# Which blocks of a later group have their sums placed on chip: second, fourth, sixth and eighth instead of first, third, sixth and eighth

## The chip, the cores and the metric

One Trainium2 chip, one of its cores. The metric is the device time of one execution in microseconds (us). TensorE is called PE (its weight loads PEld), VectorE DVE, ScalarE ACT, GpSimd POOL and SyncE SP.

## The reference, cut to what matters

One layer of a hybrid diffusion backbone for 384 tokens (128 of context, 256 latent) of width 1024: adaLN, a mixer of two branches, and a mixture of 64 SwiGLU experts (inner width 256, 8 chosen per token) with a shared expert. The change is in the experts:

```
act    = silu(einsum('nd,edf->nef', t, w_gate_e)) * einsum('nd,edf->nef', t, w_up_e) * gates[:, :, None]
routed = einsum('nef,efd->nd', act, w_down_e)
shared = (silu(t @ w_gate_s) * (t @ w_up_s)) @ w_down_s
return (routed + shared).reshape(B, T, D)
```

An expert's gate, up and down weights are 1 MB each in f32; all of them, 192 MB, are read from HBM.

## The kernel before

**Blocks and turns.** The experts are sorted by load and worked in 4 groups (NGRP) of 16 experts, each in 10 blocks (BPG, UN): a heavy block (H) has one expert with up to 128 slots, a light block (L) two experts with 64 slots each. Group 0 runs in the order HHHHLLLLLL (ORDER0), groups 1 to 3, the later ones, in HLLHLHLLHL (ORDER). One pass of one block on all engines is a turn. In turn u PE does (`block_turn`, L1519): gate and up of block u (`gate_up`, L1457), transposes of the next block's tokens (L1454), the down product of block u-1 (`down`, L1471), transposes of the activation (L1541), the slot numbers of block u+3 (L1445) and, if block u-1 is placed, its set of placing products (`place`, L1491). So block v's products stand in turn v+1.

**Two ways out of a block.** The result of a block is one row per slot; rows must be added up per token. A scattered block writes its rows with an indirect accumulating DMA from POOL (L748) into y_dram. A placed block (in later groups alone, `is_placed`, L411, by the tuple PLACED, L45) stays on chip: ACT writes the high part of its rows into y_r (`rows_out`, L1035), DVE makes a 0/1 matrix from the slots' tokens (L2007) and the low part of the rows (`place_low`, L2010), PE multiplies matrix and rows in 12 products (L1503), and DVE adds the 6 results to ffn_acc (`place_sums`, L2021). PE's next gate/up waits until the first of these is out, its next transposes until all are (L1526, L1529). `place_low` of block v waits for the scatter of block v-1, since the two use each other's buffer (L2016); `scatters_ahead` and `places_ahead` (L414, L419) count scatters and sets from PLACED, and `SCATTERED` (L46) follows from it.

**The weights.** SP issues all loads in one order (L549 to L559): in turn u gate and up of block u's experts (`load_gu`, two DMAs of 1 MB each), then down of block u-1 (`load_dn`, one). There are five buffers (RING): the heavy blocks use slot 3 alone, the light experts slots 1, 2, 4 and 0 in turn, so that two light blocks are held. A load waits on SP until the products that read the slot's former weights are done.

**After the last turn** the accumulated rows of y_dram, of the last block and of ffn_acc are added (L1566 to L1574, L2036 to L2059), and the final norm is taken.

Of the kernel before, what the change touches and what calls it, by code (L numbers as in the profile page):

```python
# [41 lines left out]
NBLK = NPASS_BLK * MAXPASS  # L42
NSIDE = 2 * NPASS_BLK
FIXED = 4
PLACED = (0, 2, 5, 7)  # L45
SCATTERED = BPG - len(PLACED)  # L46
HEAVY = 16
EMPTY = 1024
# [16 lines left out]
def hybrid_step(nc, x_prompt, x_sample, cache_k, cache_v, state_f, state_b, c, c_ctx,  # L65
# [5 lines left out]
    with ctx:  # L71
# [336 lines left out]

        assert max(PLACED) < UN - 2 and all(v + 1 not in PLACED for v in PLACED)

        def is_placed(u, first):  # L411
            return not first and u % UN in PLACED

        def scatters_ahead(b, u):  # L414

            back = 1 if u < 0 else 0
            return b * (16 * SCATTERED) + 16 * (len(PLACED) - SCATTERED * back + sum(v not in PLACED for v in range(u % UN)))

        def places_ahead(b, v, each):  # L419

            return b * (each * len(PLACED)) + each * (PLACED.index(v) - len(PLACED))

# [41 lines left out]
        def _(sp):  # L464
# [95 lines left out]

            sp.wait_ge(S["added"], passes * (NGRP * SCATTERED * 16) + 16 * (len(PLACED) - 1))
            sp.sem_inc(S["sp_turn"], 1)
# [1527 lines left out]
```

## Time and profile before

| | |
|---|---|
| three timed runs | 967.43, 969.09, 971.62 us (median 969.09) |
| the profiled execution | 965.96 us, its span 963.7 us |
| PE busy | 883.8 us, 92% |
| DVE, ACT, POOL busy | 413.2, 253.4, 144.0 us |
| SP's DMA queue (q1) | 263.21 MB, 68.7% of the span on 16 DMA engines |
| POOL's DMA queue (q0) | 27.37 MB, 10.0% |
| granted clock of PE, mean | 0.977 |

The experts run from 378 to 928 us of the span, the later groups from 508 us. In the rows, times are microseconds from the span's start. A row of the order of time gives start, duration, engine, line, operation, output and inputs, the count of instructions merged, and in brackets the idle time of the engine before it and what ended it.

### The profile page before, as it was taken

The page shows a single profiled execution, that of the slowest core. Times are in us where ns is not written, and L with a number is a line of the kernel's source. Part 1 is how long each engine was busy: PE and PEld are TensorE (multiplying, and loading weights), DVE is VectorE, ACT ScalarE, POOL GpSimd, SP SyncE. Part 2 cuts the span into 40 slices and gives each one's busy share as a digit, 9 for nine tenths or more (in the row PEclk, how much of TensorE's full clock was granted, in tenths as well). Part 3 has the DMA queues.
Part 4 walks back from the last instruction along what each step waited for, and adds up shares of the span by engine and source line. Part 5 has one row for each costly group of instructions (what it writes and reads, how often), then busy time and mean ns, then how long its engine had stood idle before and what let it go on. Part 6 is the DMA issues. An engine that isn't in the chain of part 4 may idle for free.

```text
span 963.7 us, 12124 instructions
## 1 busy us (share of the span) xinstructions
PE 883.8 (92%) x4170; PEld 514.4 (53%) x4170; DVE 413.2 (43%) x947; ACT 253.4 (26%) x415; POOL 144.0 (15%) x213
## 2 busy tenths in 40 slices
PE   4799998999999999999997999999999999999973
PEld 2387875899897764543333444444443444444431
DVE  1562483577665554233331332432342334233445
ACT  2537623344423240221211111111111111111111
POOL 7300000000001041122132012012102111111112
PEclk9799999999999999999998999999999999999987
DMA  9974778422227197799999999999999999999832
GB/s 341 343 252 182 293 262 239 109 89 79 98 89 297 64 415 316 243 340 390 404 388 386 421 403 400 410 403 394 423 404 398 404 420 401 402 406 414 340 107 101
DMA packets 85320, 295.65 MB, mean 307 GB/s; under 512 B 17370, under 2 KB 33814, under 8 KB 60320
## 3 DMA queue, kind: packets, MB, share of 16 engines
q1 hardware_dynamic: 64400, 263.21, 68.7%
q0 software_dynamic: 12176, 27.37, 10.0%
q10 hardware_dynamic: 8704, 4.54, 2.1%
q8 instruction: 25, 0.41, 0.2%
q14 instruction: 15, 0.12, 0.0%
HBM read 287.16 MB, written 22.81 MB: 322 GB/s over the span
## 4 chain that ended last, share of the span: by engine, by line
PE 67%; DMA 19%; DVE 5%; issue 3%; ACT 2%; SPq 2%; POOL 1%; ACTq 1%; POOLq 0%; DVEq 0%
PE bank L1466 21%; DMA gu<-in_w_up_e_dram 12%; PE bank L1485 10%; PE bank L1090 7%; PE bank L1092 6%; PE bank L1091 6%; DMA y_dram<-y_sb,slot_row 4%; DMA chunk_raw<-in_w_ada_dram 3%; PE bank L1503 3%; PE bank L1454 3%; PE bank L1118 2%; PE bank L1359 2%; PE bank L1159 1%; PE bank L1192 1%; PE bank L1541 1%
## 5 line engine op out<-in xcount | busy, mean ns | idle before, releaser
L1466 PE MATMUL bank<-gu,x_t 128*64 128x512 f32 (+1 forms) x1024 | 286.4, 601 | 12.8 <-DMA gu<-in_w_up_e_dram 11.0
L1466 PEld LDWEIGHTS bank<-gu,x_t 128*64 128x64 f32 (+1 forms) x1024 | 102.6, 151 | 167.7 <-issue 162.2
L1485 PE MATMUL bank<-dn,a_t 128*64 128x512 f32 (+1 forms) x512 | 145.3, 597 | 4.1 <-ACT shared_sb L1016 3.5
L1985 DVE TENSOR_TENSOR act_sb<-silu_sb,bank 128x256 f32<-128x256 f32 x40 | 16.9, 422 | 229.4 <-ACT silu_sb L1059 229.4
L1059 ACT ACTIVATE silu_sb<-bank 128x256 f32<-128x256 f32 x40 | 15.4, 385 | 330.0 <-PE bank L1466 330.0
L748 POOL DMA_INDIRECT y_dram<-y_sb,slot_row x27 | 45.9, 1701 | 306.5 <-DVE slot_row L1875 260.6
L1485 PEld LDWEIGHTS bank<-dn,a_t 128*64 128x64 f32 (+1 forms) x512 | 48.5, 150 | 74.0 <-issue 67.4
L1090 PE MATMUL bank<-h_hi,chunk_lo 128*128 128x384 f32 x240 | 84.6, 353 | 0.0
L1092 PE MATMUL bank<-h_hi,chunk_hi 128*128 128x384 f32 x240 | 81.1, 338 | 0.0
L1091 PE MATMUL bank<-h_lo,chunk_hi 128*128 128x384 f32 x240 | 81.0, 337 | 0.0
L736 POOL DMA_INDIRECT xg<-h_dram,slot_tok x42 | 44.0, 1047 | 179.8 <-DVE slot_row L1875 155.5
L443 DVE TENSOR_TENSOR chunk_lo<-chunk_raw,chunk_hi 128x2048 fp32r<-128x2048 f32 x25 | 57.1, 2287 | 19.4 <-ACT chunk_hi L437 19.3
L1993 DVE COPY a_t<-bank 128x256 f32<-128x256 f32 x40 | 17.0, 424 | 103.9 <-PE bank L1541 103.7
L437 ACT ACTIVATE chunk_hi<-chunk_raw 128x2048 fp32r<-128x2048 f32 x25 | 47.7, 1914 | 49.6 <-PE bank L1092 49.4
L1044 ACT ACTIVATE y_sb<-bank,slot_gate 128x512 f32<-128x512 f32 x56 | 38.5, 687 | 66.6 <-PE bank L1485 63.8
L1454 PEld LDWEIGHTS bank<-ident,xg 128*128 128x128 f32 x328 | 36.4, 141 | 27.9 <-issue 27.9
L1090 PEld LDWEIGHTS bank<-h_hi,chunk_lo 128*128 128x128 f32 x240 | 45.4, 189 | 7.0 <-issue 5.3
L1091 PEld LDWEIGHTS bank<-h_lo,chunk_hi 128*128 128x128 f32 x240 | 45.5, 190 | 0.3
L1092 PEld LDWEIGHTS bank<-h_hi,chunk_hi 128*128 128x128 f32 x240 | 45.5, 189 | 0.0
L2026 DVE TENSOR_TENSOR ffn_acc<-ffn_acc,bank 128x512 f32<-128x512 f32 x72 | 44.1, 682 | 0.4
L1503 PE MATMUL bank<-y_r,place_r 128*128 128x512 f32 x144 | 35.9, 398 | 8.8 <-DVE a_t L1993 6.9
L1454 PE MATMUL bank<-ident,xg 128*128 128x128 f32 x328 | 43.9, 277 | 0.0
(345 smaller groups left out, 1072.7 us busy)
## 6 DMA issues: line engine op xcount, KB each, us to landing
gu<-in_w_gate_e_dram SPq DMA_DIRECT2D x64, 1024.0 KB, 15.7
gu<-in_w_up_e_dram SPq DMA_DIRECT2D x64, 1024.0 KB, 20.8
dn<-in_w_down_e_dram SPq DMA_DIRECT2D x64, 1024.0 KB, 26.0
chunk_raw<-in_w_ada_dram SPq DMA_DIRECT2D x24, 1024.0 KB, 8.9
chunk_raw<-in_w_in_dram SPq DMA_DIRECT2D x18, 1024.0 KB, 5.4
chunk_raw<-in_w_out_dram SPq DMA_DIRECT2D x4, 1024.0 KB, 5.0
y_dram<-zeros POOLq DMA_DIRECT2D x1, 3072.0 KB, 17.6
chunk_raw<-in_w_pa_dram SPq DMA_DIRECT2D x2, 1024.0 KB, 5.0
```

Source lines behind the costliest of these rows:

```text
L437: act.activation(chunk_hi[j % HIGHS][:, :], chunk_raw[slot[n]][:, :], ACT.Copy).then_inc(S["chunk_high"], 1)
L443: dve.tensor_tensor(chunk_lo[slot[n]][:, :], chunk_raw[slot[n]][:, :], chunk_hi[j % HIGHS][:, :].bitcast(F32), ALU.subtract).then_inc(S["c ...
L736: pool.indirect_dma_start(xg[u % 2][:, :], None, h2_dram[:, :], bass.IndirectOffsetOnAxis(ap=slot_tok[:, u % UN:u % UN + 1], axis=0), boun ...
L748: pool.indirect_dma_start(y_dram[:, :], bass.IndirectOffsetOnAxis(ap=slot_row[:, u % UN:u % UN + 1], axis=0), y_sb[u % 2][:, :], None, bou ...
L1090: pe.matmul(out, left[1], right[0], start=start, stop=False)
L1091: pe.matmul(out, left[0], right[1], start=False, stop=False)
L1092: return pe.matmul(out, left[0], right[0], start=False, stop=stop)
L1454: mm = pe.transpose(bank[k // 4][:, (k % 4) * P:(k % 4 + 1) * P], xg[u % 2][:, k * P:(k + 1) * P], ident[:, :])
L1466: mm = pe.matmul(bank[2 + u % 2][at_x, :].rearrange("p (g n) -> p g n", g=2), x_t[:, cols], wide[:, :, k, :], start=(k == 0), stop=(k == K ...
L1485: mm = pe.matmul(bank[5 + half][at_x, :], a_t[:, cols], dn[slot_of(x, first)][:, wc], start=(k == 0), stop=(k == 1))
L1503: return pe.matmul(out[:, :], place_r[:, t * P:(t + 1) * P], y[:, halves[half]], start=start, stop=not start)
L2026: dve.tensor_tensor(ffn_acc[t][:, cols], ffn_acc[t][:, cols], out[:, :], ALU.add).then_inc(S["place_out"], 1)
```

## The change

The tuple that says which blocks of a later group are placed is another one. Nothing else is edited; the counts of scatters and sets, the waits and the turns in which sets, scatters and sums stand are computed from it.

```
-PLACED = (0, 2, 5, 7)
+PLACED = (1, 3, 5, 7)
```

In each later group the four sets of products stood in turns 1 (light), 3 (heavy), 6 (light) and 8 (heavy); they now stand in turns 2 (light), 4 (light), 6 (light) and 8 (heavy). Blocks 0 and 2 become scattered, blocks 1 and 3 placed; the placed ones are two heavy and two light, as before, and the six scattered ones are 0, 2, 4, 6, 8, 9 instead of 1, 3, 4, 6, 8, 9.

## Rows read from the trace of the kernel before

**Rows 1.** The page: span, and DMA busy tenths in 40 slices of it

```profile
span 963.7 us, 12124 instructions
...
DMA  9974778422227197799999999999999999999832
```

**Rows 2.** Busy by stretch: length, busy PE, PEld, DVE, ACT, POOL; PEclk, DMA share, GB/s

```profile
651.75:789.09 137.34, 131.11 (x567) 59.76 (x565) 47.53 (x126) 23.59 (x41) 20.18 (x16) 1.00 1.01 406
789.09:924.65 135.56, 131.17 (x567) 59.81 (x565) 48.08 (x129) 24.14 (x41) 20.15 (x16) 1.00 0.92 368
...
764.00:772.00 8.00, 8.00 (x32) 3.70 (x32) 1.44 (x3) 1.15 (x3) 1.97 (x2) 1.00 0.99 365
836.00:844.00 8.00, 7.25 (x38) 3.72 (x37) 4.36 (x13) 2.36 (x4) 0.00 (x0) 1.00 0.97 371
```

**Rows 3.** Order of time on PE: gate/up of turns 2.1 to 2.6

```profile
665.60 7.09 PE L1466 MATMUL bank<-gu,x_t 128*64 128x512 f32 x32 [1.78 <-DMA gu<-in_w_up_e_dram]
...
681.14 7.09 PE L1466 MATMUL bank<-gu,x_t 128*64 128x512 f32 x32
...
693.19 7.11 PE L1466 MATMUL bank<-gu,x_t 128*128 128x512 f32 x16
...
708.92 7.09 PE L1466 MATMUL bank<-gu,x_t 128*64 128x512 f32 x32
...
720.61 7.11 PE L1466 MATMUL bank<-gu,x_t 128*128 128x512 f32 x16
...
734.23 7.09 PE L1466 MATMUL bank<-gu,x_t 128*64 128x512 f32 x32 [1.56 <-DMA gu<-in_w_up_e_dram]
```

**Rows 4.** Order of time on PE: gate/up of 3.1, 3.2, 3.4, 3.5 and 3.6

```profile
802.14 7.09 PE L1466 MATMUL bank<-gu,x_t 128*64 128x512 f32 x32 [0.99 <-DMA gu<-in_w_up_e_dram]
...
817.65 7.09 PE L1466 MATMUL bank<-gu,x_t 128*64 128x512 f32 x32
...
845.42 7.09 PE L1466 MATMUL bank<-gu,x_t 128*64 128x512 f32 x32
...
857.11 7.11 PE L1466 MATMUL bank<-gu,x_t 128*128 128x512 f32 x16
...
869.11 7.09 PE L1466 MATMUL bank<-gu,x_t 128*64 128x512 f32 x32
```

**Rows 5.** PE's waits, 651.7 to 924: us in total, times, longest

```profile
PE bank L1503 <- DVE a_t L1993: 4.5, 6, 0.8
PE bank L1466 <- DMA gu<-in_w_up_e_dram: 4.3, 3, 1.8
```

**Rows 6.** SP's issues, us to landing: gate/up of 3.4, then down of 3.1

```profile
L509 SPq DMA_DIRECT2D gu<-in_w_up_e_dram x2: 2055/2146/2236, 810.5 to 815.0; - x2
...
DMA to landing us min/median/max: 21.5/24.5/27.6
...
L520 SPq DMA_DIRECT2D dn<-in_w_down_e_dram x2: 361/361/361, 793.1 to 793.6; - x2
...
DMA to landing us min/median/max: 28.5/28.5/28.5
```

**Rows 7.** Scatter of block 1 in group 2; all scatters 665 to 832; DVE's low half

```profile
694.63 1.70 POOL L748 DMA_INDIRECT y_dram<-y_sb,slot_row  x1 [13.50 <-DVE slot_row L1875]
...
DMA to landing us min/median/max: 9.1/9.3/9.5
...
704.15 0.75 DVE L2018 SCALAR_TENSOR_TENSOR y_r<-bank,slot_gate,y_r 128x512 fp32r<-128x512 f32 x1 [1.92 <-DMA y_dram<-y_sb,slot_row]
```

**Rows 8.** Turn 1.1 in order of time; stretches of [rows 2]'s view around its wait

```profile
525.95 9.56 PE L1466 MATMUL bank<-gu,x_t 128*64 128x512 f32 x32 [5.61 <-DMA gu<-in_w_up_e_dram]
...
520.34:525.95 5.61, 0.00 (x1) 0.03 (x1) 1.43 (x7) 0.27 (x1) 2.70 (x2) 0.84 1.02 427
524.00:531.00 7.00, 5.05 (x12) 1.64 (x14) 0.00 (x0) 0.00 (x0) 0.66 (x1) 0.51 1.02 361
```

## The prediction

> **What bounds the kernel now.** I read the page's slices first, then busy time by stretch, then PE's order of time in the second and third later groups, then the landings. The slices show DMA at 9 tenths from slice 19 to slice 37, with PE at 9 too [rows 1]. In the two last groups the 16 DMA engines are occupied for 1.01 of the period of group 2 and 0.92 of that of group 3, which holds the end of the loading; PE is busy 131.1 us in each [rows 2]. So both run at their limit, and the question is which one is late at each turn. "Turn g.u" below is turn u of group g, counted by the start of its gate/up matmuls (L1466).
>
> PE waits for gate/up weights before turn 2.1 (1.78 us), before 2.6 (1.56) and before 3.1 (0.99) [rows 3, 4]. These three are all the waits for gate/up in the two groups, 4.3 us [rows 5]; after 802.14, the start of turn 3.1, PE alone sets the end. From the wait that ended before 2.1 to the one before 3.1, SP's queue carried 48 transfers of 1 MB (16 experts, gate, up and down) in 802.14 - 665.60 = 136.54 us [rows 3, 4], 2.84 us each. The queue never emptied as a whole (share 1.01 [rows 2]; it can pass 1, as packets overlap), so I treat the landings as a clock that PE can't hurry.
>
> **Part 1: what moves on PE.** The twelve products of a set (L1503) and the wait ahead of them lie behind the down product of the turn. Lengths of turns, from start to start, waits for weights taken off:
> - light after heavy, no set: 708.92 to 720.61, 11.69 [rows 3];
> - light after light, no set: 681.14 to 693.19, 12.05 [rows 3];
> - heavy after light, no set: 720.61 to 734.23 less 1.56, 12.06 [rows 3];
> - light after heavy, with a set: 665.60 to 681.14, 15.54 [rows 3];
> - heavy after light, with a set: 693.19 to 708.92, 15.73 [rows 3].
>
> Light after light with a set doesn't occur. Its bounds are 12.05 + (15.54 - 11.69) = 15.90 and 12.05 + (15.73 - 12.06) = 15.72; I take 15.7, since the down product ahead of the set is the same light one as in the heavy turn. Before, turns 1 to 4 take 15.54 + 12.05 + 15.73 + 11.69 = 55.01. After, they take 11.69 + 15.7 + 12.06 + 15.54 = 54.99. PE's own work is therefore unchanged. What changes is when PE stands at each turn: turn 2 is reached 3.85 us earlier, turn 3 at the same time, turn 4 3.7 us earlier, turn 5 at the same time. A set that was done while the weights came in is now ahead of PE's next need.
>
> **Part 2: can the weights follow?** SP's order is: gate/up of turn u, then down of turn u-1. After turn 1's gate/up come 5 transfers up to the end of turn 2's (one down, four gate/up), 10 more up to turn 4's, 9 more up to turn 6's, 24 more up to the next turn 1's. By 2.84 us each that is +14.2, +42.6 and +68.2 from turn 1. Landings bear this out. The second down transfer issued at 793.6 landed 28.5 us later, at 822.1; it stands two transfers behind turn 3.2's gate/up, which so landed near 822.1 - 5.7 = 816.4, against 802.0 + 14.2 = 816.2. The first expert of 3.4 was issued by 810.5 and landed 27.6 later, at 838.1; the second, two transfers on, near 843.8, against 844.6 by the clock [rows 4, 6].
>
> Now the slack. Turn 3.2 started at 817.65 [rows 4]; its weights were there at 816.3, 1.3 us ahead. With PE there 3.85 us earlier, PE waits 2.5 us. Turn 3.4 started at 845.42; its weights came between 843.8 and 844.6, so 0.8 to 1.6 us ahead, and an arrival 3.7 us earlier would wait as well. The wait is new, and it isn't given back: behind it comes the set, which before was done in the shadow of the same transfers.
>
> **Part 3: the ledger.** Group 2: turn 2.1 starts at 665.60 as before (the wait of 1.78 us ahead of it takes up the delay that group 1 hands on, which by the steps below is 1.6). PE is at 2.2 at 677.3; weights at 665.5 + 14.2 = 679.7; start 679.8. 2.3 at 695.5 (was 693.19). 2.4 at 707.6, weights at 708.1, start 708.2. 2.5 at 723.7 (was 720.61). 2.6 at 735.8: the weights' wait that ended at 734.23 is gone, and PE is 1.6 us late. The rest keeps its lengths, so 3.1 is reached at 801.15 + 1.6 = 802.75, where the weights are there since 802.0: +0.6. Group 3: 3.2 reached at 814.4, weights at 816.3, start 816.4. 3.3 at 832.1 (was 829.7 by the same lengths). 3.4 reached at 844.2, weights between 843.8 and 844.6, start 844.4. 3.5 at 859.9, against 857.11: +2.8 [rows 4]. From there nothing waited for gate/up weights [rows 5] and nothing is moved, so +2.8 goes through to the end; I round to +3.0, since the second landing may be the later bound.
>
> **Part 4: what else is moved.** Scatters of blocks 1 and 3 become those of 0 and 2: one turn earlier each, the same number per group (six), and by turns 4 and 6 the same count has passed. POOL's queue: each scatter goes out about 1.4 us into the turn after the next one (694.63 for block 1, turn 2.3 began at 693.19) and lands 9.1 to 9.5 us later; behind it stands only the gather of a block two turns ahead [rows 7]. Three scatters now follow one another (8's to 0's), at turn distances of 11.7 us and more, over the 9.5 of a landing. DVE's low half of block v waits for the scatter of block v-1: in turn 2.3 this cost DVE 1.92 us [rows 7], and behind it on DVE stands a_t (L1993), for which PE waits ahead of its set: 4.5 us in six sets [rows 5], 0.75 each, inside the lengths above. The moved scatter of block 0 goes out near 678.7, just ahead of 2.2's landing at 679.7; between none of it and, at the dearest, one transfer's 2.84 us could fall on that landing. I take none, since only 1 of its 9.3 us lies ahead of the landing, and keep +1 in the range.
>
> On how the moved scatter shares the engines, the row shows a scatter landing in 9.3 us while SP's transfers took 24 to 28 [rows 6, 7]: it doesn't queue behind them. The Trainium skill, "DMA: Bandwidth & Descriptors", section "Queues, rings and completion order", says that each DMA engine serves its queues in turn, packet by packet; the trace agrees. By it the moved scatter takes its share from turn 2's weights at once, which makes the wait longer, not shorter.
>
> SP: the heavy turn 3's gate/up now ends 2.3 us later, and with it the release of slot 3. The DMA share in the 8 us around that release, 836 to 844, is 0.97, and 0.99 around the release for turn 3.0, 764 to 772 [rows 2]; so a few of the 16 engines ran out already. Bound: 0.04 of 8 us, 0.3 us, up to the whole 2.3 if all ran out. The weights behind it are turn 6's, which PE now reaches 1.6 to 2.8 us after their landing, so this is covered; without the cover it would be up to +1.
>
> **The sum.** The profiled execution took 965.96 us with a span of 963.7. Plus 3.0 is 969.0. The median of the three timed runs, 969.09, is 3.13 above it, and the prediction is for that: 972.1 us.
>
> **The rivals.**
> - *Clock.* In the wait of 5.61 us before turn 1.1 the granted clock fell to half, and the gate/up of that turn took 9.56 us where 7.09 is usual, 2.47 more [rows 8]. The waits of 1.78 and less left it at 1.00. The new waits before 2.2 and 3.2 are 2.0 to 2.5 us, between the two and nearer to those that did nothing. A fall at 2.2 is taken up again: group 2 then ends 1.9 us later still, 3.2 is reached at 816.3 and finds its weights without a wait, and 3.3 starts at 832.0 as forecast. It costs if it comes at 3.2: 3.3 at 834.6, 3.5 at 862.2, +5.1, 974.2 us. The Trainium skill, "TensorE: Matmul & The Clock Gate", section "HAM oscillation — how this bites in real kernels", tells of a kernel in which every wait for a tile's DMA brought the clock down; by that rule this is what happens here, at every new wait.
> - *The set waits for the scatter.* Turns 2 and 4 come right after scatters, and in group 3 each delay of DVE's low half goes to the end. At up to 1.9 us in each of two turns beyond the lengths taken: +3.8 on top, 975.9 us. Against it: the heavy turn's length of 15.73 already has this wait.
> - *No change.* PE's sums are equal; if the landing of 3.2 and 3.4 is some 2.5 us earlier than my clock says, there is no new wait: 969.1. Against it: two landings agree with it within 1 us. That the new tuple isn't used is no rival: every count on scatters and sets is computed from it.
> - *Faster.* Turn 1 without a set releases nothing earlier, but turn 2's down and gate/up are one set ahead, so SP's issues for turns 4 and 6 are earlier. It decides if the DMA engines lose time now for want of issues: 0.01 to 0.04 of 8 us in two places a group [rows 2], under 1 us in all, and the wait of 0.99 before 3.1. Price: 1 to 2 us, 967.5.
>
> **How the numbers follow.** A measurement here can tell about 0.5%, 4.85 us, from no change. Chances: forecast (970.3 to 974) 0.58, clock 0.10, scatter 0.11, no change 0.15, faster 0.06. Slower by over 0.5% takes scatter and most of clock: 0.20. Faster by over 0.5% needs more than the fourth rival gives: 0.04. The rest, 0.76, is within. The range reaches down to 967.5 (no change and most of the gain, the three runs spread by 4 us) and up to 976.5 (scatter).
>
> **What would show it.** PE's order of time after: turns 2.2 and 3.2 preceded by an idle of about 2 us that gu's DMA ends, the wait before 2.6 gone, the sets of turns 2 and 4 at 15.5 to 15.9, group 3 from 3.1 to 3.5 near 57.2 where it was 54.97. Wrong, if these idles are missing, or if their sum is above 5 us a group (then the weights came later than their clock), or if a gate/up of 9 us stands behind them.

## The result

| | before | after |
|---|---|---|
| median of 20 timed runs | 965.3 us | 968.34 us |
| lowest and highest | 962.62 to 971.62 | 965.94 to 974.26 |
| ratio after/before | | 1.0034, 95% interval 1.0019 to 1.0049 |
| the profiled execution's span | 963.7 us | 971.0 us |
| start of turn 1.0 to the end of the span | 455.4 us | 458.3 us |

The change costs 3.0 us, a third of a per cent, clear of the noise of twenty runs. The forecast started from a base of 969.09 us, the median of three runs; the median of twenty lies 3.8 us below it, so those three were high. The two profiled spans differ by 7.3 us, but 4.4 of these lie ahead of the later groups, where nothing was changed (turn 1.0 starts at 508.28 and at 512.69). From there on it is 2.9 us.

The order of time on PE of the changed kernel, gate/up and sets of group 2 and of group 3 from turn 1 on:

```profile
669.98 7.09 PE L1466 MATMUL bank<-gu,x_t 128*64 128x512 f32 x32 [0.69 <-DMA gu<-in_w_up_e_dram]
...
684.92 8.78 PE L1466 MATMUL bank<-gu,x_t 128*64 128x512 f32 x32 [3.10 <-DMA gu<-in_w_up_e_dram]
...
699.56 2.97 PE L1503 MATMUL bank<-y_r,place_r 128*128 128x512 f32 x12 [0.75 <-DVE a_t L1993]
702.36 7.03 PE L1466 MATMUL bank<-gu,x_t 128*128 128x512 f32 x16
...
714.27 7.09 PE L1466 MATMUL bank<-gu,x_t 128*64 128x512 f32 x32
...
726.90 3.01 PE L1503 MATMUL bank<-y_r,place_r 128*128 128x512 f32 x12 [0.80 <-DVE a_t L1993]
729.75 7.03 PE L1466 MATMUL bank<-gu,x_t 128*128 128x512 f32 x16
...
808.49 7.09 PE L1466 MATMUL bank<-gu,x_t 128*64 128x512 f32 x32
...
820.70 7.09 PE L1466 MATMUL bank<-gu,x_t 128*64 128x512 f32 x32 [0.38 <-DMA gu<-in_w_up_e_dram]
...
848.77 7.09 PE L1466 MATMUL bank<-gu,x_t 128*64 128x512 f32 x32 [0.34 <-DMA gu<-in_w_up_e_dram]
...
864.19 7.03 PE L1466 MATMUL bank<-gu,x_t 128*128 128x512 f32 x16
```

Turn 2.2 now waits 3.10 us for its weights, where [rows 3] show it starting at 681.14 with no wait. In group 3 the waits stand before 3.2 and 3.4, 0.38 and 0.34 us. The wait of 1.56 us before turn 2.6 [rows 3] is gone. PE's waits over groups 2 and 3 of the changed kernel (us in total, times, longest):

```profile
PE bank L1503 <- DVE a_t L1993: 4.6, 6, 0.8
PE bank L1466 <- DMA gu<-in_w_up_e_dram: 4.5, 4, 3.1
```

Its busy time by stretch (group 2, group 3, the wait before 2.2, the matmuls behind it; columns as in [rows 2]):

```profile
657.23:796.50 139.27, 132.56 (x567) 60.43 (x565) 47.44 (x126) 23.58 (x41) 20.18 (x16) 0.99 1.01 406
796.50:931.60 135.10, 130.97 (x567) 60.06 (x565) 48.08 (x129) 24.14 (x41) 20.12 (x16) 1.00 0.90 361
681.80:684.90 3.10, 0.01 (x1) 0.00 (x0) 1.45 (x7) 0.46 (x1) 1.60 (x1) 1.00 1.02 427
685.00:689.00 4.00, 4.00 (x12) 1.24 (x14) 0.00 (x0) 0.00 (x0) 1.04 (x1) 0.57 1.02 394
```

The sum of the waits for weights, 4.5 us, is hardly more than the 4.3 of [rows 5]. What counts is where they stand. Before, a wait of 1.56 us stood at turn 2.6 and one of 0.99 at 3.1; now the long one stands at 2.2 with the set still to come, and the clock fell behind it: 0.57 granted in the next 4 us, so 1.2 GHz for most of them and 2.4 for the rest, and a gate/up of 8.78 us instead of 7.09. PE is busy 1.5 us longer in group 2 (132.56 against 131.11 in [rows 2]); the fall alone is 8.78 - 7.09 = 1.69 us. The DMA engines are as full as before, 1.01.

Counted from the start of turn 1.0, turn 3.1 comes 1.9 us later than before (808.49 - 512.69 = 295.8, against 802.14 - 508.28 = 293.9), turn 3.5 comes 2.7 us later, and the end 2.9 us.

### The profile page after: what moved, and what is told of

The parts are those of the page before. It is cut to its first block, busy times and chain, and to the rows that moved or that the text cites. A ratio compares the mean times of both kernels' runs of the same rounds, so it can differ in the third digit from the quotient of the medians.

```text
span 971.0 us, 12115 instructions
## 1 busy us (share of the span) xinstructions
PE 890.8 (92%) x4170; PEld 521.9 (54%) x4170; DVE 413.0 (43%) x947; ACT 253.6 (26%) x415; POOL 143.9 (15%) x213
## 4 chain that ended last, share of the span: by engine, by line
PE 69%; DMA 18%; DVE 5%; issue 2%; ACT 2%; SPq 1%; POOL 1%; ACTq 1%; POOLq 0%; DVEq 0%
PE bank L1466 21%; DMA gu<-in_w_up_e_dram 11%; PE bank L1485 10%; PE bank L1090 6%; PE bank L1092 6%; PE bank L1091 6%; DMA chunk_raw<-in_w_ada_dram 3%; DMA y_dram<-y_sb,slot_row 3%; PE bank L1503 3%; PE bank L1454 3%; PE bank L1359 2%; PE bank L1118 2%; PE bank L1159 1%; PE bank L1337 1%; PE bank L1192 1%
## 5 line engine op out<-in xcount | busy, mean ns | idle before, releaser
L748 POOL DMA_INDIRECT y_dram<-y_sb,slot_row x27 | 45.9, 1701 | 313.4 <-DVE slot_row L1875 268.1
L1503 PE MATMUL bank<-y_r,place_r 128*128 128x512 f32 x144 | 35.9, 398 | 10.1 <-DVE a_t L1993 8.1
```

The costliest lines, as they stand in the source:

```text
L748: pool.indirect_dma_start(y_dram[:, :], bass.IndirectOffsetOnAxis(ap=slot_row[:, u % UN:u % UN + 1], axis=0), y_sb[u % 2][:, :], None, bou ...
L1503: return pe.matmul(out[:, :], place_r[:, t * P:(t + 1) * P], y[:, halves[half]], start=start, stop=not start)
```

## The experiments

The times from turn 1.0 to the end of the span, used below, leave out the early stages, whose length varied by up to 8 us among the profiled executions (turn 1.0 started between 504.7 and 512.7). They are read from one execution each and aren't exact either: two traces of one kernel gave 458.3 and 458.8 us for the changed one, but 452.3 and 455.4 us for one of those with halved loads. Most kernels have a single trace.

**Theory A**, the forecast's: weights land by a clock that PE can't hurry, and a set costs nothing where PE would otherwise wait. **Rival B**: a set in a light turn behind a light one costs more in itself. **Rival C**: the moved scatters hold up the weights of turns 2 and 4.

### The changed kernel again

The edit is the change itself.

> The changed kernel again, beside the others: sets in turns 2, 4, 6 and 8 of a later group. Theory A (weights land by a clock of 2.84 us per transfer; a set is free only where PE would otherwise wait for weights): +2.8 to +3.0 us against the kernel before, PE waits for gate/up before turns 2 and 4, none before turn 6. Rival B (a set in a light turn that follows a light turn costs PE more in itself, 1 us a group): also about +3. Rival C (the scatters of blocks 0 and 2 share the DMA engines with the weights of turns 2 and 4 and delay them): also about +3. This run is the measure for the other three.

Measured: 967.4 us (12 runs) beside 965.63 (35 runs), ratio 1.0024, 95% interval 1.0009 to 1.0040. Turn 1.0 to the end: 964.5 - 505.7 = 458.8 us. The medians are 1.8 us apart, the interval is 0.9 to 3.9 us, so the cost is there again, but its size isn't known better than that. The wait before turn 2.2 is there too, with the slowed gate/up behind it (order of time on PE):

```profile
678.09 8.78 PE L1466 MATMUL bank<-gu,x_t 128*64 128x512 f32 x32 [3.53 <-DMA gu<-in_w_up_e_dram]
```

No wait for weights stood before turn 2.4 or 3.2 in this trace, and 0.51 us before 3.4.

### Half of the change

```
-PLACED = (0, 2, 5, 7)
+PLACED = (0, 3, 5, 7)
```

> Only half of the change: PLACED = (0, 3, 5, 7), sets in turns 1, 4, 6 and 8, the scatter of block 3 replaced by that of block 2. Theory A: turn 2 is reached 15.5 us after turn 1 and finds its weights (14.2); turn 4 is reached at 15.5 + 12.05 + 12.06 = 39.6 where the weights come at 42.6, a wait of 3.0 us, then the set: turn 5 at 58.2 instead of 55.0. In group 3 this stays: +2.5 to +3.2 us in all, as much as the whole change. Rival B: no light turn after a light one has a set: 0. Rival C: one of two scatters is moved: about half, +1.5.

Measured: 968.54 us, ratio 1.0028, interval 1.0008 to 1.0049; turn 1.0 to the end 458.6 us. The order of time on PE, gate/up of 2.2, 2.4, 2.5 and of 3.1, 3.4, 3.5:

```profile
684.26 7.09 PE L1466 MATMUL bank<-gu,x_t 128*64 128x512 f32 x32
...
711.79 8.69 PE L1466 MATMUL bank<-gu,x_t 128*64 128x512 f32 x32 [3.41 <-DMA gu<-in_w_up_e_dram]
728.78 7.03 PE L1466 MATMUL bank<-gu,x_t 128*128 128x512 f32 x16
...
807.50 7.09 PE L1466 MATMUL bank<-gu,x_t 128*64 128x512 f32 x32
...
847.43 7.09 PE L1466 MATMUL bank<-gu,x_t 128*64 128x512 f32 x32 [0.33 <-DMA gu<-in_w_up_e_dram]
862.84 7.03 PE L1466 MATMUL bank<-gu,x_t 128*128 128x512 f32 x16
```

With turns 1 and 2 as before, the wait stands before turn 4: 3.41 us, where theory A put 3.0. In group 3, which was reached 2.4 us late, only 0.33 us of it was left. The whole price is paid by this one move, without any set in a light turn behind a light one, so rival B, which wanted 0, doesn't explain it. One moved scatter goes with as long a delay as two (458.6 against 458.3 and 458.8 us from turn 1.0 on), where rival C wanted half; but C's 1.5 us lies inside the interval of the timed runs.

The landings themselves decide on C. The last gate/up weights of a turn, in us from the start of turn 1.0, in the five traces with full loads that have them (that of the kernel before lacks most of these records):

| sets of blocks | 2.1 | 2.2 | 2.4 | 3.2 | 3.4 |
|---|---|---|---|---|---|
| 1, 3, 5, 7 | 157.2 | 172.2 | 200.1 | 308.0 | 335.9 |
| the same again | 156.8 | 172.3 | 200.2 | 307.9 | 336.1 |
| 0, 3, 5, 7 | 157.4 | 172.2 | 200.4 | 308.6 | 336.1 |
| 0, 2, 4, 6 | 157.0 | 172.1 | 200.3 | 308.6 | 336.1 |
| 0, 2, 4, 7 | 158.7 | 173.7 | 201.9 | 309.9 | 337.4 |

The entries of turn 2.2 in the first and the fourth row come from SP's issue of that transfer and its time to landing (changed kernel: 660.65 + 24.2 less the 512.69 of turn 1.0; sets of 0, 2, 4, 6: 658.09 + 26.4 less 512.41; the views round the issue to a tenth):

```profile
L509 SPq DMA_DIRECT2D gu<-in_w_up_e_dram x1: 381/381/381, 660.6 to 660.6; - x1
...
DMA to landing us min/median/max: 24.2/24.2/24.2
...
L509 SPq DMA_DIRECT2D gu<-in_w_up_e_dram x1: 389/389/389, 658.1 to 658.1; - x1
...
DMA to landing us min/median/max: 26.4/26.4/26.4
```

In the first two rows block 0 is scattered, 1.6 to 2.0 us ahead of the landing of 2.2; in the other three it is placed. The landing comes at the same time, within 0.3 us in four of the five traces (in the last all landings are late by some 1.4 us, from group 1 on). In the kernel with sets of 0, 3, 5, 7 block 2's scatter goes out 1.9 us ahead of the landing of 2.4, and with sets of 0, 2, 4, 6 that block is placed: 200.4 and 200.3. So the moved scatters didn't delay the weights, and rival C is out. By A the two moves don't add, since both are measured against the same landings; that is what is seen. Not every landing kept its time: those of turn 3.1 came at 291.8 to 292.1 in the first three rows and at 293.9 with sets of 0, 2, 4, 6, where PE waited for them.

### The other sets moved

```
-PLACED = (0, 2, 5, 7)
+PLACED = (0, 2, 4, 7)
```

> The other end moved: PLACED = (0, 2, 4, 7), sets in turns 1, 3, 5 and 8; block 5 scattered instead of 4. Theory A: turns 1 to 4 as before; turn 5's set comes ahead of turn 6, which is reached 70.7 us after turn 1 where its weights are there at 68.2, so the wait before turn 6 is filled by the set; turn 7 at 82.4, weights at 82.5. From turn 7 on as before: 0, within 0.7 us. Rival B: 0. Rival C: one scatter moved one turn later: 0 to -1.

Measured: 966.1 us, ratio 1.0003, interval 0.9981 to 1.0025: no difference that can be told. Groups 2 and 3 are those of before, 136.5 us from 2.1 to 3.1 and 110.1 from 3.1 to 3.9. The one profiled execution took 458.0 us from turn 1.0 on, 2.5 more than before, but that lies in group 1 (1.5) and behind the last turn (1.1), not in the groups where theory A was worked out.

This trace holds one thing more. PE's gate/up of turn 2.1, and the granted clock of the 3.8 us from its start (columns as in [rows 2]):

```profile
668.17 8.78 PE L1466 MATMUL bank<-gu,x_t 128*64 128x512 f32 x32 [2.27 <-DMA gu<-in_w_up_e_dram]
...
668.20:672.00 3.80, 3.80 (x12) 1.51 (x14) 0.00 (x0) 0.00 (x0) 1.70 (x2) 0.59 1.00 425
```

A wait of 2.27 us brought the clock down here and slowed the gate/up behind it by 1.69 us. The length of group 2 stayed that of before all the same, since the wait of 1.56 us before 2.6 was gone.

### A set in a light turn behind a light one

```
-PLACED = (0, 2, 5, 7)
+PLACED = (0, 2, 4, 6)
```

> PLACED = (0, 2, 4, 6), sets in turns 1, 3, 5 and 7; turn 7 is a light turn after a light one. Theory A: turn 7 reached at 82.4, turn 8 at 98.1, turn 9 at 110.2 us after turn 1, which in the kernel before is 110.1; weights of turn 9 are there: 0 to +0.7 us. Rival B: the light-after-light set stands in turn 7 now and costs 1 us a group as it did in turn 2: +1 to +3. Length of turn 7 tells: 15.7 by A, over 16.5 by B.

Measured: 966.96 us, ratio 1.0013, interval 0.9991 to 1.0035; turn 1.0 to the end 455.5 us, as before. Gate/up of turns 3.1, 3.6, 3.7, 3.8 and 3.9:

```profile
806.40 7.09 PE L1466 MATMUL bank<-gu,x_t 128*64 128x512 f32 x32 [3.03 <-DMA gu<-in_w_up_e_dram]
...
877.09 7.09 PE L1466 MATMUL bank<-gu,x_t 128*64 128x512 f32 x32
888.85 7.09 PE L1466 MATMUL bank<-gu,x_t 128*64 128x512 f32 x32
904.50 7.03 PE L1466 MATMUL bank<-gu,x_t 128*128 128x512 f32 x16
916.40 7.09 PE L1466 MATMUL bank<-gu,x_t 128*64 128x512 f32 x32
```

Turn 3.7 with its set takes 904.50 - 888.85 = 15.65 us, against the 15.7 of the forecast. The interval of the timed runs (-0.9 to 3.4 us) wouldn't exclude rival B's 1 to 3 us; the length of the turn does. The wait of 3.03 us before 3.1 left the next gate/up at 7.09 us.

### Weights that come early

In the next two kernels the later groups load only the first half of each down weight; the down products then read a stale second half. This part of the computation is left out in all kernels of this section. The one line more shifts the lines behind it by one (L749 is L748 of before, L1504 is L1503).

```
-                sp.dma_start(dn[k][:, :], w_down_e[0, e].rearrange("a (p k) n -> (a p) (k n)", k=2)).then_inc(dn_ready[k], 16)
+                cols = slice(0, 2048 if group is None else 1024)
+                sp.dma_start(dn[k][:, cols], w_down_e[0, e].rearrange("a (p k) n -> (a p) (k n)", k=2)[:, cols]).then_inc(dn_ready[k], 16)
```

> The kernel before with DMA's load taken down: in the later groups each down weight is loaded in its first half alone (0.5 MB instead of 1), so a group has 48 transfers' worth less 8, 40 by 2.84 = 113.7 us, against 131 us of PE work. The down products then use stale second halves; all instructions and waits of the engines stay. Theory A: the waits for gate/up after turn 1.1 vanish (5.4 us in the kernel before from turn 1.6 on), the wait before 1.1 may stay, since its weights are loaded ahead of the cut: 5 to 9 us faster than the kernel before. If PE's pace were set by other things than the landings: no change.

> The changed kernel (sets in turns 2, 4, 6, 8) with the same cut of the down loads to their first halves. Theory A: with the weights always ahead, where the sets stand makes no difference: equal to the other halved kernel within 0.7 us, no idle before turns 2 and 4. Rival B (a set in a light turn after a light one costs more in itself): still 1 us per group, about +3, above the other. Rival C (scatters delay weights): 0 too, as the weights have room.

Measured, beside 966.22 us for the kernel before: with the old sets 963.92 us, ratio 0.9977, interval 0.9956 to 0.9997; with the changed sets 959.68 us, ratio 0.9928, interval 0.9904 to 0.9953. The waits for weights were gone from group 2 on, as theory A said, and with them the loss. But the kernel with the old sets gained 2.3 us, where A wanted 5 to 9, and the two weren't equal: the changed sets were the faster ones by 4.2 us between medians (1.7 us from turn 1.0 to the end in the traces, 452.3 and 450.6). Neither A, B nor C says so. The same two once more, with a third:

> The kernel before with halved down loads in the later groups, once more, since the two halved kernels came out 4 us apart where equality was expected. Theory D (with the weights early, a set whose predecessor block was the second of two scattered in a row waits for that scatter: sets of turns 1 and 6, behind the scatters of 8 and 9 and of 3 and 4; before, the wait for weights ahead of these turns hid it): PE idles of 1.2 to 1.9 us ahead of the sets in turns 1 and 6 and 0.6 to 0.75 in turns 3 and 8, again. Rival E (the 4 us come from the early stages, which start group 1 between 504 and 513 us): the time from the start of turn 1.0 to the end is equal in the two halved kernels within 0.7 us.

> The changed kernel with halved down loads, once more. Theory D: sets in turns 2, 4, 6 and 8; behind two or three scatters in a row stands only the set of turn 2 (scatters 8, 9, 0), all later ones follow a single one, so fewer idles over 1 us ahead of sets: 2 to 4 us faster than the other halved kernel from turn 1.0 to the end. Rival E: equal.

The third has the same cut and

```
-PLACED = (0, 2, 5, 7)
+PLACED = (0, 3, 5, 7)
```

> Halved down loads with PLACED = (0, 3, 5, 7): sets in turns 1, 4, 6 and 8. Theory D: the set of turn 1 still follows two scatters in a row (8 and 9) and waits 1.2 to 1.9 us more, the set of turn 4 follows 1 and 2 and waits too, the set of turn 6 follows block 4 alone and doesn't: between the two others or like the halved kernel before. No idle for weights ahead of turn 4 (3 us with full loads). Rival E: equal to both.

| halved loads, sets of blocks | us | ratio to the kernel before, interval | turn 1.0 to the end |
|---|---|---|---|
| 0, 2, 5, 7 | 967.37 | 1.0011, 0.9987 to 1.0034 | 455.4 |
| 0, 3, 5, 7 | 963.37 | 0.9964, 0.9943 to 0.9985 | 451.6 |
| 1, 3, 5, 7 | 959.85 | 0.9942, 0.9919 to 0.9965 | 449.0 |

The old sets with halved loads, second run. The scatters of blocks 8 and 9 in order of time on POOL, and the first one's time to landing from the view of its tile:

```profile
649.73 1.62 POOL L749 DMA_INDIRECT y_dram<-y_sb,slot_row  x1 [13.30 <-issue]
662.73 1.59 POOL L749 DMA_INDIRECT y_dram<-y_sb,slot_row  x1 [10.05 <-DMA y_dram<-y_sb,slot_row]
...
DMA to landing us min/median/max: 12.1/12.1/12.1
```

DVE's low half of block 0 in turn 2.1:

```profile
672.92 0.75 DVE L2019 SCALAR_TENSOR_TENSOR y_r<-bank,slot_gate,y_r 128x512 fp32r<-128x512 f32 x1 [3.66 <-DMA y_dram<-y_sb,slot_row]
```

The sets of turns 2.1, 2.3 and 2.6 in order of time on PE:

```profile
674.35 2.98 PE L1504 MATMUL bank<-y_r,place_r 128*128 128x512 f32 x12 [2.42 <-DVE a_t L1994]
...
702.12 2.97 PE L1504 MATMUL bank<-y_r,place_r 128*128 128x512 f32 x12 [0.75 <-DVE a_t L1994]
...
742.75 2.96 PE L1504 MATMUL bank<-y_r,place_r 128*128 128x512 f32 x12 [2.21 <-DVE a_t L1994]
```

PE's waits for a_t in groups 2 and 3:

```profile
PE bank L1504 <- DVE a_t L1994: 9.8, 6, 2.4
```

The changed sets with halved loads, second run: the sets of turns 2.2, 2.4 and 2.6, and then the same waits:

```profile
684.53 2.98 PE L1504 MATMUL bank<-y_r,place_r 128*128 128x512 f32 x12 [0.75 <-DVE a_t L1994]
...
711.84 2.97 PE L1504 MATMUL bank<-y_r,place_r 128*128 128x512 f32 x12 [0.75 <-DVE a_t L1994]
...
739.13 2.99 PE L1504 MATMUL bank<-y_r,place_r 128*128 128x512 f32 x12 [0.75 <-DVE a_t L1994]
```

```profile
PE bank L1504 <- DVE a_t L1994: 4.8, 6, 1.0
```

This is theory D, and for turns 1 and 6 of groups 2 and 3 its mechanism is what the rows show. Block 8's scatter, out at 649.73, took 12.1 us to land. Block 9's had to wait for it on POOL and went out at 662.73, 2.6 us into turn 2.1. DVE's low half of block 0 waited for that one 3.66 us, a_t stood behind it on DVE, and PE stood idle 2.42 us ahead of its set. The same in turn 6, behind the scatters of blocks 3 and 4. Turns 3 and 8 follow a single scatter and have the usual 0.61 to 0.75. With the changed sets the set of turn 2 follows scatters in a row, and in turn 2.2 it waited 0.75. Rival E, the early stages, is out as the whole cause, since a gap of 6.4 us is there from turn 1.0 on; 5.5 of it lies in groups 2 and 3, and 4.6 us lay there in the first pair of traces.

D isn't complete. It wanted 2 to 4 us from turn 1.0 on, and the second pair of traces shows 6.4. With sets of 0, 3, 5, 7 it wanted an idle before the set of turn 4, behind the scatters of 1 and 2, and in turn 2.4 there were the usual 0.75 us. With the changed sets, in group 1, the sets of turns 4 and 6 waited 2.09 and 1.44 us behind single scatters. And D puts the wait down to the weights' wait that is gone alone, though block 8's scatter also took 12.1 us here against 9.6 in the kernel before; how much each of the two adds wasn't tested.

## Why the prediction was right or wrong

**The size and the sign.** Forecast +3.0 us; measured +3.04 between medians, 2.9 from turn 1.0 in the traces, and a ratio of 1.0024 in the second comparison (1.8 us between its medians). The step that failed for the absolute time is a term of *The sum*: the 3.13 us by which the median of three runs stood above the profiled execution's 965.96, taken over whole into 972.1. Twenty runs put the kernel before at 965.3, which is 0.66 below that execution. So the 968.34 measured lies 3.8 us under the forecast and under the 970.3 to 974 that were given 0.58, though inside 967.5 to 976.5; against 965.3 the 972.1 reads as a loss of 6.8 us. The chances gave most to "within 0.5%", and 0.34% is within, though it is a real loss and not noise.

**The signs that it named.** The wait before 2.2 came and the one before 2.6 was gone. But the idle of some 2 us before 3.2 was 0.38, 3.1 to 3.5 took 864.19 - 808.49 = 55.70 us and not 57.2, and a gate/up of 8.78 us stood behind the wait of 2.2, which it had called a sign of being wrong. So the +3.0 was reached by another path than the ledger's.

**Part 1, PE's own work unchanged**: right. Over both groups PE's busy time grew by 1.25 us, less than the slowed gate/up's 1.69. Turn 2.4 with its set took 729.75 - 714.27 = 15.48 us (15.54 taken), the light turn behind a light one 15.65 in the kernel with sets of 0, 2, 4, 6 (15.7 taken). By these lengths turn 4 is reached 3.9 us earlier, not 3.7 as Part 1 says (15.54 + 12.05 + 15.73 against 11.69 + 15.7 + 12.06); the ledger has it right.

**Part 2, the landings as a clock**: right in kind, its first term too small. The wait before 2.2 ended 684.92 - 669.98 = 14.9 us after 2.1 began, not 14.2. So the wait was 3.10, not 2.5. The sum of the queue over a group did hold: 136.5 us from 2.1 to 3.1 in the kernel with sets of 0, 2, 4, 7 as well. So the mean of 2.84 us a transfer held for 48 of them, while five in a row took 0.6 to 0.9 us longer than by that mean. The moved scatter isn't the cause: from landing to landing it is 15.0 us in the changed kernel and 14.8 and 15.1 in two where block 0 is placed (the table above). Why these five take longer is open. In group 3 the landings that PE met were where the forecast had them: the one of 3.4 at 336.1 us from turn 1.0 by the forecast (844.4 - 508.28) and at 335.9 in the changed kernel.

**Part 3, the ledger**, from the start of turn 1.0, less the same of before:

| turn | forecast | measured |
|---|---|---|
| 2.1 | 0 | 0.0 |
| 2.3 | +2.3 | +4.8 |
| 2.5 | +3.1 | +4.7 |
| 2.6 | +1.6 | +3.0 |
| 3.1 | +0.6 | +1.9 |
| 3.5 | +2.8 | +2.7 |
| end | +2.8, rounded to +3.0 | +2.9 |

The failing term of the ledger is group 2's, 2.5 us too small at turn 2.3: 0.7 of it the landing, 1.7 the clock. The wait of 0.5 us that it had before 2.4 didn't come, as PE was there 1.5 us after the weights. Group 2 lost 1.3 us more than forecast by its end, and the late 3.1 took that off the waits of group 3: 0.38 and 0.34 us before 3.2 and 3.4, where 2.0 and 0.2 were forecast. So the end depends little on what group 2 loses: 3.2 and 3.4 are set by landings, and only the stretch from 3.4 on adds to the end. There PE starts 1.06 us earlier than before (336.08 against 337.14 us from turn 1.0), and the set of turn 3.4 makes the turn 3.73 us longer (15.42 against 11.69): +2.67 at 3.5. This term was forecast right, and that is why two errors in group 2 didn't reach the total.

**The clock.** Counted as a rival with a chance of 0.10, since the new waits of 2.0 to 2.5 us were called nearer to those that did nothing. It fell behind the wait of 3.10 us, behind 3.53 in its second run, and behind 3.41 in the kernel with sets of 0, 3, 5, 7 (gate/up 8.78, 8.78 and 8.69 us instead of 7.09). But it also fell behind 2.27 us in the kernel with sets of 0, 2, 4, 7 (8.78), and behind an idle of 1.90 us ahead of a set with halved loads (the set took 4.29 us instead of 2.98), and not behind 2.81 and 3.03 us in the kernel with sets of 0, 2, 4, 6 (7.09). So the length of one wait doesn't tell whether the clock falls, and the chance was too low for waits of 2.0 to 2.5 us too. The price was 1.6 to 1.7 us once, where 2.47 were taken from the fall before 1.1; that a fall in turn 2.2 is taken up again by group 3 was right. The Trainium skill, "TensorE: Matmul & The Clock Gate", section "HAM oscillation — how this bites in real kernels", tells of a kernel in which every DMA wait brought the clock down. Here not every one did: the waits of 0.38 and 0.34 us before 3.2 and 3.4, and the 3.03 us above, left the next gate/up at 7.09 us.

**The scatter.** This is where the reasoning was on the wrong side. The forecast looked for a wait on the scatter in the new places, at up to 3.8 us. None came: PE's waits for a_t are 4.6 us in all against 4.5. The rows of before showed 1.92 us of it on DVE in turn 2.3 [rows 7], and the lengths of turns 1 and 3 [rows 3] were taken to hold the whole price of a set there. But turns 1 and 6 stand behind a wait for weights [rows 3, 4], in which the late scatter had time to land. Take the wait for weights away, as the halved kernels do, and PE stands idle 1.2 to 3.0 us ahead of the old sets in turns 1 and 6 (all but turn 1.1), where 0.75 is usual, and 0.6 to 1.3 us ahead of the new ones in groups 2 and 3. In these kernels the change gained 4.2 and 7.5 us between medians; with full loads it costs 3. That the wait for weights hid all of this gain isn't shown, since the halved kernels also had slower scatters.

**Where the loss comes from** is shown for the weights: one move of a set ahead of a wait gives the whole price (sets of 0, 3, 5, 7), a move behind it gives none (0, 2, 4, 7 and 0, 2, 4, 6), and with early weights the loss is gone. That the moved scatter adds to the landing of turn 2 is ruled out by the landings: 172.2 and 172.3 us with it, 172.2 and 172.1 without. The prediction's sentence that the scatter takes its share from these weights at once and makes the wait longer isn't borne out. With full loads no arrangement tried was faster than the kernel before.

## What to carry to other kernels

When two engines run level, write down for each step when the other one's goods arrive, and put movable work behind the steps that wait, not ahead of them; the sums of the work were equal here and told nothing. A wait also hides what happens under it: before an operation's length is carried to another place, look what stood idle just ahead of it. A delay early in a paced stretch can be given back (4.8 us at turn 2.3 were 1.9 at 3.1), so price the last stretch with care, in which nothing waits any more. And take the base of a forecast from more than three runs when the effect is as small as their spread.

## What the runs showed of the hardware

- Accumulating scatters of up to 128 rows of 4 KB landed in 9.1 to 9.5 us with the weights' queue at full load [rows 7]. With half the down loads the times spread: between turns 2.0 and 3.9 from 4.9 to 12.4 us, those of blocks 8 and 3 at 12.1 to 12.4 in the second run with the old sets. Why some took longer though less was moved is open.
- Taking a sixth of the later groups' weight traffic away (8 of 48 transfers) gave 0.2% at first and nothing (1.0011, interval 0.9987 to 1.0034) in the second comparison with the old sets; the waits for weights were gone from group 2 on, and longer waits ahead of the sets had come. With the changed sets it made 0.6 to 0.7% against the kernel before.
- PE's granted clock fell (0.57 over the 4 us behind the wait of 3.10 us, 0.59 over the 3.8 us behind that of 2.27) after waits of 2.27, 3.10, 3.41 and 3.53 us between dense matmuls, and the next gate/up was 1.6 to 1.7 us longer each time; it stayed at 1.00 behind waits of 2.81 and 3.03 us.
- The profiled executions start the later groups between 504.7 and 512.7 us with the same instructions ahead of them, so spans of single executions can't be compared to better than some us. Stretches from turn 1.0 on are better, but differed by 3 us in one pair of traces of the same kernel.
